# Small experts' weight units placed one by one, in place of two by two, between the large experts' units

## The reference, cut to what matters

```python
DEPTH, SEQ, D_MODEL, D_FF, N_EXPERTS, TOP_K = 2, 256, 1024, 2816, 8, 2

def swiglu(x, w1, w3, w2):
    return (jax.nn.silu(x @ w1) * (x @ w3)) @ w2

def moe(hn, w_router, w1, w3, w2):
    t = hn.reshape(B * S, D)
    logits = (t @ w_router).astype(jnp.float32)
    top_v, top_i = lax.top_k(logits, TOP_K)
    top_w = jax.nn.softmax(top_v, axis=-1)
    combine = jnp.sum(jax.nn.one_hot(top_i, N_EXPERTS) * top_w[..., None], axis=1)
    out = jnp.zeros_like(t)
    for e in range(N_EXPERTS):
        out = out + combine[:, e:e + 1] * swiglu(t, w1[e], w3[e], w2[e])
    return out
```

## Time and profile before

| | before |
|---|---|
| median of 3 runs (lowest to highest) | 1240.68 us (1237.93 to 1241.63) |
| the profiled execution's own time | 1240.51 us |
| its span, first to last instruction | 1238.9 us |
| PE busy | 1214.2 us, 98% |
| DVE busy | 816.3 us, 66% |
| ACT busy | 663.0 us, 54% |
| mean DMA rate over the span | 318 GB/s |

### The profile page before, as it was taken

How to read it: one execution, slowest core, us unless ns; L and a number is a source line. 1 busy time by engine, 2 the same in 40 slices (tenths; PEclk the granted TensorE clock), 3 DMA queues, 4 the chain that set the end, 5 groups by cost and what they waited for, 6 DMA issues and landing times. The chain is left out here.

```text
span 1238.9 us, 15727 instructions
## 1 busy us (share of the span) xinstructions
PE 1214.2 (98%) x6167; PEld 933.2 (75%) x6167; DVE 816.3 (66%) x788; ACT 663.0 (54%) x682; POOL 81.1 (7%) x76
## 2 busy tenths in 40 slices
PE   9999999999999999999999999999999999999994
PEld 8778888888888878888777776667777666777761
DVE  6867766656455766769776776666766676676632
ACT  7567445444336566457565555555555555555520
POOL 0600002000001501010000000000000000000000
PEclk9999999999999999999999999999999999999999
DMA  9753448745545454459999999999999999999996
GB/s 378 291 204 132 174 170 313 298 176 198 188 152 207 169 172 154 161 202 346 421 420 421 420 422 419 403 422 421 421 420 422 421 418 411 423 422 421 420 418 244
DMA packets 56734, 393.73 MB, mean 318 GB/s; under 512 B 6704, under 2 KB 6704, under 8 KB 11632
## 3 DMA queue, kind: packets, MB, share of 16 engines
q1 hardware_dynamic: 53104, 374.84, 76.0%
q0 software_dynamic: 3408, 17.57, 3.8%
q10 hardware_dynamic: 144, 0.26, 0.1%
HBM read 386.35 MB, written 13.64 MB: 323 GB/s over the span
## 5 line engine op out<-in xcount | busy, mean ns | idle before, releaser
L558 DVE TENSOR_TENSOR wl<-raw,wh 128x2048 fp32r<-128x2048 f32 x251 | 577.3, 2302 | 293.9 <-ACT wh L547 293.3
L547 ACT ACTIVATE wh<-raw 128x2048 fp32r<-128x2048 f32 x251 | 481.0, 1918 | 327.9 <-PE ps L565 178.5
L563 PE MATMUL ps<-wh,XT_h 128*128 128x512 f32 x944 | 375.5, 398 | 0.3 <-DVE wl L558 0.3
L565 PE MATMUL ps<-wh,XT_l 128*128 128x512 f32 x944 | 368.3, 390 | 0.0
L564 PE MATMUL ps<-wl,XT_h 128*128 128x512 f32 x944 | 367.7, 390 | 0.0
L563 PEld LDWEIGHTS ps<-wh,XT_h 128*128 128x128 f32 x944 | 177.3, 188 | 45.1 <-issue 8.6
L565 PEld LDWEIGHTS ps<-wh,XT_l 128*128 128x128 f32 x944 | 177.2, 188 | 38.0
L564 PEld LDWEIGHTS ps<-wl,XT_h 128*128 128x128 f32 x944 | 177.4, 188 | 34.6
L1690 PE MATMUL ps<-raw,few_X 128*64 128x256 f32 x1056 | 123.9, 383 | 4.1 <-DMA raw<-in_units 4.0
L1690 PEld LDWEIGHTS ps<-raw,few_X 128*64 128x64 f32 x1056 | 72.8, 137 | 49.7 <-issue 14.4
L563 PE MATMUL ps<-wh,moe_gT_h 128*128 128x512 f32 x220 | 88.4, 402 | 0.0
(11 more groups left out here) (288 smaller groups left out, 974.6 us busy)
## 6 DMA issues: line engine op xcount, KB each, us to landing
raw<-in_units SPq DMA_DIRECT2D x350, 1024.0 KB, 10.3
x_rows<-in_zeros POOLq DMA_DIRECT2D x8, 512.0 KB, 8.9
y_rows<-in_zeros POOLq DMA_DIRECT2D x6, 512.0 KB, 20.0
raw<-in_boot SPq DMA_DIRECT2D x5, 512.0 KB, 7.2
y_rows<-xs POOLq DMA_DIRECT2D x5, 512.0 KB, 8.2
back<-x_rows POOLq DMA_DIRECT2D x4, 512.0 KB, 9.2
h<-in_x SPq DMA_DIRECT2D x1, 1024.0 KB, 12.7
rows<-in_rows SPq DMA_DIRECT2D x1, 896.0 KB, 17.3
```

What stands on the lines that cost most here:

```text
L547: nc.scalar.activation(wh[:, U.split_slot(j), :], raw[:, U.raw_slot(j), :], ACT.Copy).then_inc(hi_ready, 1)
L558: nc.vector.tensor_tensor(wl[:, s, :], raw[:, U.raw_slot(j), :], wh[:, s, :].bitcast(F32), ALU.subtract).then_inc(lo_ready, 1)
L563: nc.tensor.matmul(o, xh, bh, start=start, stop=False)
L565: return nc.tensor.matmul(o, xl, bh, start=False, stop=stop)
```

## The change

A light unit is put into both lists as soon as one is due, in place of two as soon as two are due. The rule for its place stays: ahead of the last two heavy units in `IN_USE`, behind them in `LOADED`.

```diff
         due = max(0, n + 1 - FEW_FROM) * (len(few) - FEW_ALONE) // (len(chain) - FEW_FROM)
-        while due - done >= 2:
-            two = few[done:done + 2]
-            loaded += two
-            used[-2:-2] = two
-            done += len(two)
+        while due - done >= 1:
+            one = few[done:done + 1]
+            loaded += one
+            used[-2:-2] = one
+            done += 1
     return loaded + few[done:], used + few[done:]
```

## The result

The changed kernel takes 1245.54 us (median of 4 runs, 1244.71 to 1245.75) against 1240.09 us for the kernel before on the same chip (4 runs, 1237.93 to 1241.63): a ratio of 1.005 with a 95% interval of 1.0038 to 1.0062, 5.4 us more. It is slower, by 0.4 to 0.6%: more than the 0.3% (3.7 us) that the prediction took as the least that a measurement of this kernel can tell. The profiled executions took 1240.51 us before and 1245.71 us after.

The account below looks back on a forecast made before the run. The DMA was taken to set the pace, PE having 5.5 to 8 us of slack; PE's added work, partly absorbed, delays expert 7, and the tail adds +2.0 us to 1240.51: 1242.5 us, range 1239.5 to 1247.0.

Parts of the forecast that it names:

- the price on PE: Expert stage: splitting a pair of light units costs PE 0.37 us; 44 added blocks make +16.3 us of PE time.
- +13.9 us: PE's whole added work: 16.3 us for split pairs, less 2.0 and 0.4 us for cheaper transposes.
- the slack: PE's spare time in the DMA-paced stage, 5.5 to 8 us, absorbs part of 15.6 us; expert 7 ends 7.6 to 10 later.
- the cost of the loads in the stage: Expert stage loads: PE's lag eats the DMA's backlog only near the end, so it was costed at nothing.
- the cover: The DMA's backlog of at least one load in the stage; without it each late slot costs up to its own lateness.
- the tail: After expert 7: last loads wait for later slots, so loads and gathers finish at 1228.2 us, not 1226.2: +2.0 us.
- the likeliest case: The forecast itself, whole run: +1 to +4 us, own range 1241 to 1244.5 us, chance 0.45.
- the second rival: Stage: PE becomes the bound, its 5.5 us of waits stay, expert 7 ends 15.6 us later; 1245.9 us, chance 0.27.
- Same: Whole run: a time within about 0.3%, 3.7 us, of no change; chance 0.64, against slower 0.30 and faster 0.06.
- signs of being wrong: Light units wait for landings as often as before, last gather before 1226, or stage DMA rate well under 415 GB/s.
- The third rival: Stage start, 555 to 580 us: light slots freed earlier let loads start earlier, up to 4 us faster, 1236.5; chance 0.06.
- the fourth: PE in the stage: switches between kinds cost nothing new, 1240.5 us; chance 0.22 together with the first rival.

Follow-up runs that it names:

- pairs_switch: Kernel before, light units still in pairs, with two short light-kind matmuls added inside one heavy unit of each of the 43 heavy runs: 1251.63 us.
- second_half1: Kernel before with light units by pairs for the first 44 and singly from the 45th on: 1244.03 us, ratio 1.0022 to 1.0047.
- first_half1: Kernel before with the first 44 light units placed singly and the later ones by pairs: 1240.34 us, ratio 0.9997 to 1.0015.
- ones_less: Changed kernel with one of four input-channel chunks left out of each of the small experts' 66 gate and up units: 1239.04 us.

## Why the prediction came out as it did

**Right: the price on PE.** 0.37 us for each pair that is split was worked out, and the changed kernel shows the 2.54 us for a single unit that it rests on. Removing 14 us of PE work takes the change back, which fits the +13.9 us.

**Right: the slack.** 15.6 us up to the end of expert 7 less 5.5 to 8 of slack gave 7.6 to 10; the store came 8.3 later, so 7.3 were taken up. The waits for landings went to zero and PE was busy 605.50 of 606 us, as forecast.

**Wrong: the cost of the loads in the stage.** The prediction said that PE's lag "eats that backlog near the end and no earlier, so I cost this at nothing". The changed kernel's DMA is under its rate as early as 740 us. Three of its windows, and one from between them:

```profile
740.00:790.00 50.00, 49.75 (x224) 32.16 (x223) 32.92 (x25) 26.26 (x23) 1.60 (x3) 1.00 1.00 408
840.00:890.00 50.00, 50.00 (x277) 36.39 (x276) 35.59 (x26) 26.96 (x21) 0.00 (x0) 1.00 1.01 421
990.00:1040.00 50.00, 50.00 (x227) 32.36 (x225) 33.75 (x23) 27.18 (x22) 0.00 (x0) 1.00 1.01 410
1040.00:1090.00 50.00, 50.00 (x253) 34.92 (x252) 29.88 (x17) 27.73 (x20) 1.67 (x3) 1.00 1.00 407
```

The kernel before, in the three low ones:

```profile
740.00:790.00 50.00, 49.28 (x224) 32.56 (x223) 34.76 (x26) 26.66 (x22) 0.54 (x1) 1.00 1.01 418
990.00:1040.00 50.00, 50.00 (x232) 35.03 (x232) 34.00 (x24) 29.53 (x25) 0.00 (x0) 1.00 1.01 418
1040.00:1090.00 50.00, 49.26 (x263) 35.11 (x262) 31.21 (x18) 26.00 (x19) 1.67 (x3) 1.00 1.01 418
```

The time is lost in patches (also from 1140 to 1190 us: 407 against 421), and between them the changed kernel's rate is 420 to 421, as before. What sets their places was not traced. Past some lag a late PE makes a load late, by the chain of ACT's waits shown above, and a DMA that has no slack cannot make it up: even between the patches it moves no more than 421 GB/s. That this lag is set by the three places of `wh` and the six of `raw` is read from the program and was not varied. This term was 5.0 us, by the bytes, where the prediction had 0. The prediction did say what would follow if the cover were gone (each late slot costs the DMA up to its own lateness); it gave it no part of the sum. The times from issue to landing were to shrink toward 5 us late in the stage. They did so early as well: the shortest was 5.5 us before 790 us, and 7.1 behind 1100. The DMA share hardly shows any of this: in the windows above it stays at 1.00 or 1.01.

**Mis-sized: the tail.** It was forecast to end at 1228.2 and ended at 1232.4. The sum started from a DMA with nothing left to do at 1205.9 and left out the store's own 0.5 MB (1.25 us); in the run the loads were still behind from the stage. The slots of the last loads did come late, as said, and the DMA slowed down while it waited for them:

```profile
1204.00:1208.00 4.00, 4.00 (x27) 1.67 (x23) 0.78 (x3) 0.97 (x3) 0.54 (x1) 1.00 0.94 367
1208.00:1212.00 4.00, 4.00 (x19) 1.35 (x20) 0.88 (x5) 0.22 (x1) 0.00 (x0) 1.00 0.88 301
```

Against 419 that is 4 x 52 + 4 x 118 = 680 KB less, 1.6 us. The kernel before was not full to the end either, so the two tails have to be compared whole: 11.38 MB from 1196 to 1226.2 us before, 13.26 MB from 1196 to 1232.4 us after, which is 3.0 and 4.8 us over what the bytes need at 419 GB/s. The tail so adds 1.8 us to the 5.0 of the stage, 6.8 against the 6.2 us by which the last gather was late. Part of that was given back behind it (span +5.2), where the output's last transfer landed in 3.1 us in place of 4.2.

**The forecast as a whole.** 1242.5 us was forecast and 1245.5 measured, inside the range (1239.5 to 1247.0) and above the likeliest case's own (1241 to 1244.5). The direction and the mechanism on PE were foreseen. That the time still fell inside the range is owed to the range's width, which the second rival had set, and not to the sum. "Same" had the largest chance, 0.64, and by the prediction's own measure of 3.7 us it is "slower", which had 0.30. Of its signs of being wrong none came up, the rate only just: 416 GB/s in the stage where "well under 415" was asked. The second rival named nearly the right time (1245.9) but for another reason: it wanted new waits for landings at the single units and expert 7 late by 15.6 us, and there were no such waits, and 8.3. The third rival (faster through slots freed earlier) is excluded by the result, the fourth (the changes of kind cost nothing) by pairs_switch. The rule of the Trainium skill on the change of tiling mode ("TensorEngine Tiling (Array Packing)", Key Properties) agrees with these traces in direction; whether it is the tiling or the change of the operands' type, from the float32r of heavy units to the float32 of light ones, that costs the 0.37 us was not told apart.

## What to carry to other kernels

Where two resources are both full, ask of each added us not only whether the other one's waits can cover it, but where in time these waits lie: here slack ahead of the added work was lost (second_half1), and slack behind it was used (first_half1). And where the two share rings of few places, look for where the one that falls behind delays the other. Here the DMA did not catch up, and its busy share still read 100%, so sum up its bytes over the stage. Read also on whom the engine between them waits: ACT's waits turned from landings to PE. Finally, price the boundary between two kinds of matmul before work is interleaved finely; blocks of two and of three took the same time here.

## What the runs showed of the hardware beyond that

Near the end of the changed kernel, around its longest pause for a landing, PE's granted clock fell. PE's timeline, and the windows (the last three columns are the clock, the DMA share and GB/s):

```profile
1219.45 1.94 PE L1690 MATMUL ps<-raw,few_gT 128*64 128x512 f32 x8 [0.32 <-DMA raw<-in_units]
1224.44 3.06 PE L1690 MATMUL ps<-raw,few_gT 128*64 128x512 f32 x8 [3.06 <-DMA raw<-in_units]
1228.20 5.69 PE L1690 MATMUL ps<-raw,few_gT 128*64 128x512 f32 x16 [0.70 <-DMA raw<-in_units]
```

```profile
1224.00:1228.00 4.00, 3.06 (x8) 0.70 (x8) 0.00 (x0) 0.00 (x0) 0.00 (x0) 0.64 1.01 418
1228.00:1232.00 4.00, 3.73 (x10) 0.94 (x11) 0.00 (x0) 0.00 (x0) 0.00 (x0) 0.51 0.40 162
```

Behind pauses of 0.32 and then 3.06 us the mean clock of a window was 0.51, the lower of the two levels (1.2 GHz), and a light unit's 8 matmuls took 3.06 us in place of 1.94. In the kernel before, four pauses of up to 2.1 us in the same place left the clock at 1.00. It cost nothing here: the last gather landed at 1232.4 us, DVE was adding the gathered rows until 1237.6, and PE's last matmuls for the small expert's part, 1234.79 + 1.99 = 1236.8, ended ahead of that.

Also, a float32 matmul is two records in the profile: the 86 short matmuls added to pairs_switch are 172 records. So the "16 matmuls" of a light gate or up unit are 8 matmuls of the program, the "8" of a down unit are 4, and a chunk that ones_less left out was 0.43 us and not 0.21.
